# Where a VectorE accumulates two early conditioning vectors, and where TensorE turns three of them into columns

## The reference

```python
for l in range(DEPTH):
    sh_m, sc_m, gt_m, sh_f, sc_f, gt_f = [t[:, None] for t in
                      jnp.split(silu_c @ w_mod[l] + b_mod[l], N_MOD, axis=-1)]
    ux = modulate(x, g[0], sh_m, sc_m)
    if is_attn:
        # k_c, v_c from the context, window attention with all context keys, 2-D DFT of 4 channel groups
        mix_x = jnp.concatenate([fourier_mix(f_x), attn_x], axis=-1) @ w_out
    else:
        mix_x = short_conv_mix(ux, conv_w_in[m], conv_w[m], conv_w_out[m])
    x = x + gt_m * rmsnorm(mix_x, g[1])
    x = x + gt_f * rmsnorm(sq_relu_mlp(modulate(x, g[2], sh_f, sc_f), mlp_w1[l], mlp_w2[l]), g[3])
```

## Time and profile before

| | us |
|---|---|
| median of 3 runs | 2384.14 (2377.64 to 2387.01) |
| profiled execution, its own time | 2381.69 |
| its span, first to last instruction | 2379.9 |
| TensorE matmul busy | 2239.5 |
| VectorE busy | 1656.3 |
| ScalarE busy | 993.0 |
| mean granted TensorE clock | 0.97 of full |

### The profile page before, as it was taken

How to read it: one execution, slowest core, us unless ns; L and a number is a source line. 1 busy time by engine, 2 the same in 40 slices (tenths; PEclk the granted TensorE clock), 3 DMA queues, 4 the chain that set the end, 5 groups by cost and what they waited for, 6 DMA issues and landing times.

```text
span 2379.9 us, 31101 instructions
## 1 busy us (share of the span) xinstructions
PE 2239.5 (94%) x11455; PEld 1833.0 (77%) x11455; DVE 1656.3 (70%) x1780; ACT 993.0 (42%) x1211; POOL 140.8 (6%) x43
## 2 busy tenths in 40 slices
PE   6889978969999999999979999996999999999998
PEld 3477645758888888888868788875888888888886
DVE  0264633878879878878888998787887655555565
ACT  2173531434434434434444344443443443443443
POOL 0000000010102101100110110011010100000000
PEclk8899998979999999999999999998999999999999
DMA  9945965848888888888867787774888666666764
GB/s 376 351 151 202 361 244 175 296 154 269 284 290 280 277 294 284 282 297 292 287 234 248 264 294 271 250 268 157 274 281 295 187 191 189 193 189 193 204 192 141
DMA packets 253897, 592.63 MB, mean 249 GB/s; under 512 B 18083, under 2 KB 18611, under 8 KB 253235
## 3 DMA queue, kind: packets, MB, share of 16 engines
q1 hardware_dynamic: 253746, 590.63, 73.8%
HBM read 588.46 MB, written 2.10 MB: 248 GB/s over the span
## 4 chain that ended last, share of the span: by engine, by line
PE 79%; DVE 7%; DMA 7%; issue 3%; ACT 2%; POOL 1%; SPq 1%; DVEq 0%; ACTq 0%; POOLq 0%
PE ps L497 26%; PE ps L498 13%; PE ps L560 10%; PE ps L562 10%; PE ps L561 10%; DMA mraw<-in_w_mod_dram 3%; DVE wlo L1129 2%; PE ps L453 2%; DVE acc L1139 2%; DMA early<-in_w_mod_dram 2%; PE ps L524 1%; ACT whi L827 1%; DMA raw<-in_conv_w_in_dram 1%; DMA raw<-in_mlp_w_dram 1%; PE ps L683 1%
## 5 line engine op out<-in xcount | busy, mean ns | idle before, releaser
L1129 DVE TENSOR_TENSOR wlo<-raw,whi 128x1024 fp32r<-128x1024 f32 x712 | 925.9, 1307 | 476.7 <-ACT whi L827 471.5
L827 ACT ACTIVATE whi<-raw 128x1024 fp32r<-128x1024 f32 x712 | 749.6, 1058 | 978.3 <-PE ps L562 375.4
L497 PE MATMUL ps<-u,whi 128*128 128x512 f32 x2944 | 1040.2, 398 | 12.9 <-DVE wlo L1129 10.2
L498 PE MATMUL ps<-u,wlo 128*128 128x256 f32 x2944 | 825.3, 280 | 0.0
L497 PEld LDWEIGHTS ps<-u,whi 128*128 128x128 f32 x2944 | 554.3, 188 | 152.7 <-issue 12.1
L498 PEld LDWEIGHTS ps<-u,wlo 128*128 128x128 f32 x2944 | 557.3, 189 | 0.2
L560 PE MATMUL ps<-whi,h 128*128 128x512 f32 x1216 | 477.2, 392 | 18.2 <-DVE wlo L1129 16.2
L561 PE MATMUL ps<-wlo,h 128*128 128x512 f32 x1216 | 475.3, 391 | 0.0
L562 PE MATMUL ps<-whi,h 128*128 128x512 f32 x1216 | 475.3, 391 | 0.0
L1139 DVE SCALAR_TENSOR_TENSOR acc<-mraw,cs,acc 128x1024 f32<-128x1024 f32 x240 | 313.3, 1305 | 3.9 <-DMA mraw<-in_w_mod_dram 3.8
L560 PEld LDWEIGHTS ps<-whi,h 128*128 128x128 f32 x1216 | 229.7, 189 | 70.0 <-DVE wlo L1129 18.8
(11 more groups left out here) (184 smaller groups left out, 1260.8 us busy)
## 6 DMA issues: line engine op xcount, KB each, us to landing
raw<-in_mlp_w_dram SPq DMA_DIRECT2D x512, 512.0 KB, 4.6
mraw<-in_w_mod_dram SPq DMA_DIRECT2D x272, 512.0 KB, 5.2
early<-in_w_mod_dram SPq DMA_DIRECT2D x96, 512.0 KB, 7.0
raw<-in_conv_w_in_dram SPq DMA_DIRECT2D x96, 512.0 KB, 5.6
raw<-in_att_w_in_dram SPq DMA_DIRECT2D x40, 512.0 KB, 4.2
raw<-in_att_w_out_dram SPq DMA_DIRECT2D x32, 512.0 KB, 6.3
raw<-in_conv_w_out_dram SPq DMA_DIRECT2D x32, 512.0 KB, 5.7
raw<-in_w_mod_dram SPq DMA_DIRECT2D x16, 512.0 KB, 6.8
```

What stands on the lines that cost most here:

```text
L497: pe.matmul(bank, whi[:, s % SLOTS, cols], src[:, k, :], start=(k == 0), stop=False)
L498: last = pe.matmul(bank[:, 0:T], wlo[:, s % SLOTS, cols], src[:, k, 0:T], start=False, stop=(k == KC - 1))
L827: act.activation(whi[:, s, :], raw[:, s, :], ACT.Copy).then_inc(hi_ready, 1)
L1129: dve.tensor_tensor(wlo[:, s, :], raw[:, s, :], whi[:, s, :], ALU.subtract).then_inc(lo_ready, 1)
```

## The change

VectorE's units 0 and 1 begin earlier. `first_unit_slab(0)` to (11) follow `lo` of slabs 12 to 23 (the last query slabs and K/V), (12) to (14) follow `lo` of slabs 24 to 26, and (15) follows that; 16 to 31 stand in steps 0 to 15, one each, and no step from 16 on has any. SyncE's order of loads is moved to match. The mix units are made in the order 2, 3, 4 in place of 3, 4, 2, so that the row of unit 2 is there after step 8. Each of the three sets of columns now stands at the end of one of TensorE's steps 21, 22 and 23, and writes to another PSUM bank (2 in place of 6). `spread_gate(0)` stands where it was, ahead of the second slab of the output projection, but waits for VectorE's `finish_first`, and GpSimd's first sum no longer waits for it.

```diff
-MIX_UNITS = (3, 4, 2)
+MIX_UNITS = (2, 3, 4)
...
-            for w in range(SLOTS, W_F + 6):
+            for w in range(SLOTS, SL):
                 att_slab(w)
             first_unit_slab(0)
             first_unit_slab(1)
+            for w in range(SL, W_F + 6):
+                att_slab(w)
+                if w >= 2 * SL:
+                    first_unit_slab(w - 2 * SL + 2)
             for t in range(-1, 17):
                 att_slab(W_F + t + 7)
                 if t == -1:
                     sp.wait_ge(slab_used, W_KV + SL)
                 mix_pair(t + 1)
-                if t >= 0:
-                    first_unit_slab(t + 2)
+                if t < 14:
+                    first_unit_slab(t + 18 - (t < 0))
+                if t == -1:
+                    first_unit_slab(17)
             for t in range(17, 23):
                 mix_pair(t + 1)
-                first_unit_slab(2 * t - 15)
-                first_unit_slab(2 * t - 14)
-            first_unit_slab(31)
...
+            def unit_columns(un):
+
+                src, pick = ((acc[:, 0, :], ones[:, 0:2]), (acc[:, 1, :], ones[:, 0:2]), (mix_row[0], sel))[un]
+                for c in range(KC // 2):
+                    last = pe.matmul(ps[:, 2, 16 * un + 2 * c:16 * un + 2 * c + 2], src[:, c * P:(c + 1) * P],
+                                     pick, start=True, stop=True)
+                if un == 2:
+                    last.then_inc(columns_done, 1)
...
+                if t == 21:
+                    pe.wait_ge(pt_copied, 2 * HEADS)
+                    pe.wait_ge(m_used, DVE_FIRST * UNIT)
+                    pe.wait_ge(mix_copied, 1)
+                if t >= 21:
+                    unit_columns(t - 21)
...
                 if s == 1:
-                    unit_columns()
-                    pe.wait_ge(pt_copied, 2 * HEADS)
+                    pe.wait_ge(mod_ready, 3)
                     spread_gate(0, 2)
...
                 if s == SL // 2 + 1:
-                    pe.wait_ge(mod_ready, 3)
+                    pe.wait_ge(mix_copied, 3)
                     spread_gate(1, 6)
...
                     lo(SL * (i + 1) + s, s % SLOTS)
+                    if i or s >= 4:
+                        first_unit_slab(8 * i + s - 4)
...
             for s in range(3):
                 lo(W_F + s, s)
+                first_unit_slab(12 + s)
+            first_unit_slab(15)
...
-                for m in first_unit_slabs(t):
-                    first_unit_slab(m)
+                if t < UNIT:
+                    first_unit_slab(UNIT + t)
...
-            pool.wait_ge(gate_spread, 1)
             for un in range(POOL_FIRST, len(UNITS)):
```

More of the change, by code:

```diff
@@ L734, in spread_gate @@
                 for n in range(2):
-                    last = pe.matmul(ps[:, bank + n, :], first_row, mix_row[i][:, n * 512:(n + 1) * 512],
+                    last = pe.matmul(ps[:, bank + n, :], first_row, mix_row[1 + i][:, n * 512:(n + 1) * 512],
                                      start=True, stop=True)
                 last.then_inc(gate_spread, 1)
[L739 to L748, removed]
             def out_waits(s):
@@ L1419, in finish_first @@
                     dve.tensor_tensor(vt[:, col:col + KC // 2],
-                                      ps[:, 6, 16 * un:16 * un + 16].rearrange("p (c w) -> p c w", w=2)[:, :, 0],
+                                      ps[:, 2, 16 * un:16 * un + 16].rearrange("p (c w) -> p c w", w=2)[:, :, 0],
                                       bT[:, col:col + KC // 2], ALU.add).then_inc(mod_ready, 1)
@@ L1753, in mix_slabs @@
     return range(2 * (t - 1), 2 * t) if 1 <= t < 23 else range(44, 48) if t == 23 else ()
-def first_unit_slabs(t):
-    return (t,) if t < 16 else range(2 * t - 16, 2 * t - 14) if t < 24 else ()
 LOAD_CTX, LOAD_X = 3, 5
```

## The result

The changed kernel takes 2348.2 us (median of 4 runs, 2344.32 to 2349.75), the kernel before 2383.48 (4 runs, 2377.64 to 2387.01). The ratio is 0.9852, 95% interval 0.9828 to 0.9876: 35.3 us less. In two later groups of runs it was 0.9864 (0.9845 to 0.9884) and 0.9851 (0.9831 to 0.987), 32.1 and 34.8 us less.

What follows compares the result with a forecast made beforehand. A chain of waits, VectorE idle until a slab landed in `mraw`, was taken to bound steps 16 to 23. -36.1 + 1.0 + 2.0 + 1.0 = -32.1 us gave 2349.6 or 2352.0, stated as 2351, range 2343 to 2366.

Steps and rivals of the forecast that it cites:

- Steps 16 to 23 and the columns: From step 16 to the second `spread_gate`: 68.5 us in place of 104.6, so 36.1 us less.
- the last mix pair: Late steps: used in the same step as the pair before it, so late by 1 to 2 us; 1.0 charged.
- The cause of the wait: Steps 16 to 23: VectorE idle for `mraw` nine times, 50.6 us, with two products a step and two slots.
- The columns: Among DFT products in steps 21 to 23: 1.95 us a set, 5.9 in all, and `spread_gate(0)` 1.9.
- the rival of low clock within the steps: Steps 21 to 23: two-column matmuls pull the clock down there too, 8 us more, 2359; chance 0.14.
- The query stage: Ahead of `lo` of slab 14: two products, 0.75 and 1.28, make it 2.0 us later, all on the path.
- the clock 1.0: After TensorE's longer wait for slab 14: work lost to a lower clock, 0 to 1.9 us, taken as 1.0.
- the two early loads: At the start: the first two `mraw` loads cost nothing; with cover gone they would cost 3 us.
- The signs named in advance: In the trace: step 16 near 310, second `spread_gate` near 379, no VectorE wait on `mraw` after step 15.
- The likeliest case: Whole kernel: the forecast itself holds, 2345 to 2358 us; chance 0.66.
- the slow chain: Steps 16 to 23: ScalarE's or the mix slabs' chain replaces `mraw`'s, 2 us a step, 16 back, 2367; chance 0.09.
- the stall in K/V: Before K/V ends: late landings make VectorE's products stall TensorE, 2396 us or more; chance 0.03.

Runs made afterwards that it cites:

- e1: The changed kernel with all 24 column matmuls back behind the first slab of the output projection, VectorE's products still moved: 2352.78 us, ratio 0.9877.
- e2: The kernel before with one edit: in steps 17 to 22 SyncE issues the two `mraw` loads ahead of the mix pair: 2356.77 us, ratio 0.9894.
- e3: The changed kernel with VectorE's first 16 products begun two slabs later, the first behind `lo` of slab 14: 2349.32 us, ratio 0.9868.
- e4: The changed kernel with its first two products behind `lo` of slab 11, in VectorE's gap, the others behind slabs 14 to 26: 2342.95 us, ratio 0.9844.
- e0: The changed kernel run again with no edit: 2348.14 us, ratio 0.9864.

## Why the prediction was right

2351 us were forecast, 2348.2 measured. The price of each stage was right to about 2 us. The cause given for the waits was incomplete, which did not enter the sum, and part of the remaining distance is scatter: of the profiled pair, 3.2 us lie outside the stages that were priced. By its steps:

- **Steps 16 to 23 and the columns.** 68.5 us were laid out in place of 104.6, and 1.0 charged for the last mix pair; D is 67.48. The layout held because nearly every part was priced start to start at full clock and the next chain was checked: it had less than a microsecond of room in step 17, and no wait shows. The last mix pair was not late, so this 1.0 was wrong here; e1 shows that it is the columns ahead of it that give it time, and that without them it costs 1.6. The other 1.0 lies in two terms: the three sets were priced at 1.95 with the tail of the last matmul, 5.9 in all, and start to start they take 5.4; the first `spread_gate` and the four slabs behind it were laid out at 13.1 and take 12.65.
- **The cause of the wait.** Here the reason was incomplete. I put the wait down to two slots and a load that waits for the slab two before. e2 shows that the larger part was the place of that load behind a mix pair in SyncE's queue: the order alone is worth 23.3 us. The rest of the change, the products' move above all, is worth 32.2 (D of e1 against before), the columns' place 4.9 more (D of the changed kernel against e1: 3.2 of clock, 1.6 of the mix pair), together 37.1. The new order of the mix units and GpSimd's missing wait are in the 32.2 and were not run alone. The forecast of the move's effect did not depend on the cause, since the move takes the loads away together with their place in the queue. As far as the cause goes this is luck: for a change of SyncE's order alone, the same reason would have forecast little or nothing.
- **The columns.** 1.95 a set and 1.88 for the `spread_gate` came as forecast; the rival of low clock within the steps did not come. e1 and e2 show it where the sets stand together. But the gain was put down to the columns' place alone, and the low clock before had two causes. From the first set to the second `spread_gate` it was 24.63 us before, where full clock gives 18.1. With the waits ahead gone and the columns in the old place it is 21.28 (e1) and 21.31 (e2). So about half of the 6.6 us comes back with the waits, and the other half with the new place. One argument against the rival rested on a single sample: the set behind an idle 1.13 us (L464) took 1.95 in six of the ten traces, and 2.32 to 2.46 in the others.
- **The query stage.** 2.0 us were forecast for the two products ahead of slab 14; Q grew by 1.87. For the clock 1.0 was charged between 0 and 1.9; KV grew by 1.2 and 1.5 us in two executions of the changed kernel and by nothing in the third. The upper bound of 1.9 came from a single sample as well: over the same window, 128 to 140 us, the granted clock was 0.84 before and 0.73 in the changed kernel's trace, and the 0.64 read beside it is from 124 to 128 us, nearly all of it the wait itself. e3 and e4 undo the growth of Q by the order alone.
- **K/V and the early steps.** TensorE had no gap in K/V, S did not change (95.44 to 95.27), and e0 shows no price for the two early loads. The signs named in advance are there: step 16 begins at 310.74, the second `spread_gate` at 378.22, and VectorE does not wait for `mraw` after step 15.
- **The likeliest case and its rivals.** The time fell in the likeliest case's own range, 2345 to 2358; the slow chain and the stall in K/V did not appear in the changed kernel, though e3 shows how near the latter is: with 16 products begun two slabs later, the last one comes late.

## What to carry to other kernels

When an engine waits for a load, look at what the load's own queue was waiting for: a transfer with a free slot may stand behind another that waits for the very engine which is stalled, and one line in another place can be worth most of a rebuild (23.3 of 37.1 us here). Look also at whether the engine that sets the pace depends on this wait: the same exchange in steps 0 to 13 took some 12 us of waits from VectorE and nothing from the time. Hide extra work in a gap that the timeline shows (here behind slab 11), not at the slab where the engine is already the one waited for. And spread very narrow matmuls among dense ones instead of collecting them.

## What the runs showed of the hardware that I had not expected

TensorE's granted clock fell from full speed to 0.57 (which is mostly the level of 1.2 GHz) while the engine was busy 4.00 of 4 us without idle time, on matmuls two columns wide: the first two sets took 3.63 us, the third alone 3.37 in e1 and 3.53 in e2. In the changed kernel the sets, with at least 4.6 us from the start of the dense matmuls behind one to the start of the next, ran at 1.00 throughout.

After a wait of 2.2 to 3.2 us in the query stage the half clock came in three executions (waits of 2.24, 2.77 and 3.15 us, KV 53.2 to 53.5) and did not in two (2.38 and 2.42 us, KV 51.9 and 52.0). The length of the wait alone does not decide it: 2.24 had it and 2.42 had not.
